# Second expert layer of a two-block kernel: own sums behind own down products, the last pair gathered in round 2, the first triple's gate products ahead of its up products

## What is computed

```python
def hier_moe(x, ...):                 # x: 256 tokens x 1024
    g_sel = argmax(x @ router_group_w + b)          # one of 4 groups
    top_logit, top_local = top_k(e_logits[g_sel], 2) # 2 of its 8 experts
    weight = p_group * softmax(top_logit)
    # every token goes to its 2 of 32 experts
    hid = silu(xb @ expert_w_gate[e]) * (xb @ expert_w_up[e])   # 1024 -> 256
    yb = hid @ expert_w_down[e]                                 # 256 -> 1024
    y = zeros.at[token].add(yb * weight)
x = layer_norm(DEEPNORM_ALPHA * x + hier_moe(x), ln2_w, ln2_b)
```

## Time and profile before

| | |
|---|---|
| time, three runs | 1296.77, 1297.43 (median), 1298.36 us |
| profiled execution: its time, its span | 1297.06 us, 1295.3 us |
| granted TensorE clock, mean | 0.940 |
| PE busy / PE weight loads / DVE / ACT / POOL | 1104.0 / 618.2 / 398.8 / 202.7 / 123.2 us |
| chain that ended last, by engine | PE 61%, DMA 31%, DVE 4%, ACT 2% |
| second experts' refills, rate of the 16 DMA engines in slices 34 to 39 of 40 (1068.6 to 1262.9 us) | 416, 421, 420, 420, 421, 419 GB/s |

### The profile page before, as it was taken

One profiled execution on the slowest core, in us unless ns is written; L12 is line 12 of the kernel. 1 busy time (PEld: TensorE's weight loads), 2 busy tenths in 40 slices (PEclk: granted clock), 3 DMA queues, 4 the chain that ended last, 5 costly groups with the idle time before them and its releaser, 6 DMA issues.

```text
span 1295.3 us, 19542 instructions
## 1 busy us (share of the span) xinstructions
PE 1104.0 (85%) x8698; PEld 618.2 (48%) x8698; DVE 398.8 (31%) x816; ACT 202.7 (16%) x420; POOL 123.2 (10%) x148
## 2 busy tenths in 40 slices
PE   7989997986667766776699999999999969998986
PEld 6645554432222222222264555888878544443432
DVE  4255843111001000100028827543185351011003
ACT  3221422010000000000000012211131032222121
POOL 0010000010003891000005610000000000000000
PEclk9999997999788778878899999999999989999988
DMA  9422848999999999999962353211313889999991
GB/s 331 150 90 107 351 197 332 427 427 428 427 429 427 426 428 427 428 427 428 414 221 98 130 211 105 107 67 67 132 65 130 327 332 416 421 420 420 421 419 45
DMA packets 62407, 377.45 MB, mean 291 GB/s; under 512 B 6128, under 2 KB 7664, under 8 KB 37104
## 3 DMA queue, kind: packets, MB, share of 16 engines
q1 hardware_dynamic: 60736, 369.64, 70.1%
q10 hardware_dynamic: 1584, 6.51, 1.4%
HBM read 375.09 MB, written 1.05 MB: 290 GB/s over the span
## 4 chain that ended last, share of the span: by engine, by line
PE 61%; DMA 31%; DVE 4%; ACT 2%; SPq 1%; issue 1%; DVEq 0%; ACTq 0%
DMA arena<-in_w_expert_up 21%; PE psum L489 11%; PE psum L492 9%; PE psum L2807 5%; DMA arena<-in_expert_w_up 4%; PE psum L1393 3%; PE psum L855 3%; PE psum L2273 3%; DMA arena<-in_w_expert_gate 3%; PE psum L1423 2%; PE psum L2495 2%; PE psum L2358 2%; PE psum L1102 2%; DMA arena<-in_w_expert_down 2%; PE psum L2818 2%; PE psum L2797 2%
## 5 line engine op out<-in xcount | busy, mean ns | idle before, releaser
L1393 PE MATMUL psum<-arena 128*32 128x256 f32 x2048 | 153.0, 449 | 91.3 <-DMA arena<-in_w_expert_up 54.5
L489 PE MATMUL psum<-arena 128*128 128x512 f32 x352 | 157.6, 598 | 3.2 <-ACT arena L526 1.6
L1393 PEld LDWEIGHTS psum<-arena 128*32 128x32 f32 x2048 | 70.8, 124 | 174.0 <-DMA arena<-in_w_expert_up 71.7
L1423 PE MATMUL psum<-arena 128*32 128x512 f32 x512 | 125.0, 640 | 17.2 <-DMA arena<-in_w_expert_down 11.9
L492 PE MATMUL psum<-arena 128*128 128x256 f32 x544 | 122.9, 382 | 1.0 <-ACT arena L1830 1.0
L492 PEld LDWEIGHTS psum<-arena 128*128 128x128 f32 x544 | 101.5, 189 | 16.9 <-issue 2.2
L489 PEld LDWEIGHTS psum<-arena 128*128 128x128 f32 x352 | 64.8, 190 | 81.4 <-issue 81.1
L2807 PE MATMUL psum<-arena 128*32 128x512 f32 (+2 forms) x672 | 82.4, 624 | 13.1 <-DMA arena<-in_expert_w_up 10.3
L1423 PEld LDWEIGHTS psum<-arena 128*32 128x32 f32 x512 | 31.4, 116 | 98.6 <-issue 71.1
L1454 DVE TENSOR_TENSOR arena<-arena,psum 128x256 f32<-128x256 f32 x16 | 6.8, 422 | 221.3 <-ACT arena L1437 221.3
L1561 POOL TENSOR_TENSOR arena<-arena 128x16 f32<-128x16 f32 (+6 forms) x64 | 43.6, 682 | 151.7 <-DMA arena<-in_ssm_bc 146.8
(11 more groups left out here) (482 smaller groups left out, 1229.7 us busy)
## 6 DMA issues: line engine op xcount, KB each, us to landing
arena<-in_w_expert_gate SPq DMA_DIRECT2D x32, 2048.0 KB, 25.2
arena<-in_w_expert_up SPq DMA_DIRECT2D x32, 2048.0 KB, 26.2
arena<-in_w_expert_down SPq DMA_DIRECT2D x31, 2048.0 KB, 25.0
arena<-in_w_in SPq DMA_DIRECT2D x21, 2048.0 KB, 8.9
arena<-in_expert_w_gate SPq DMA_DIRECT2D x32, 1024.0 KB, 19.5
arena<-in_expert_w_up SPq DMA_DIRECT2D x32, 1024.0 KB, 21.6
arena<-in_expert_w_down SPq DMA_DIRECT2D x32, 1024.0 KB, 23.3
arena<-in_w_out SPq DMA_DIRECT2D x4, 2048.0 KB, 7.8
```

What stands on the lines that cost most here:

```text
L489: mm = pe.matmul(o, lhs[:, k, sub * P:(sub + 1) * P], w[:, k, :], start=(k == 0), stop=(k == kt - 1))
L1393: mm = pe.matmul(ps[32 * c:32 * c + 32], xin[:, e, k], w[:, j, 256 * n:256 * n + 256], start=(k == 0), stop=(k == KD - 1))
L1423: mm = pe.matmul(y_ps[at:at + 32, 512 * n:512 * n + 512], hid_T4[:, j, half], w[:, j, 512 * n:512 * n + 512], start=(half == 0 and j == 0) ...
```

## The change

- Each `r2_tokens` signal now comes after each of the eight scalings. PE's wait in front of `either` is gone; in `few` the first products wait for one token part at a time, in `many` the wait for all eight stands before `begin_sums`.
- Round 0's products (`first_products_in`) are 256 wide: first all of gate, signalling the new `m2_gate`, then all of up, signalling `m2_in`. SP's `ins(2)` sends its three gate loads after `m2_gate`, its three up loads after `m2_in`.
- In rounds 0 to 8 `add(u)` comes directly after `out_of(u)`; there is nothing left between `gather_for(u+1)` and `turn_of(u)` (but `begin_sums` in round 0).
- The pair's tokens are gathered in round 2 (`SPARE`), between `turn_of(2)` and `out_of(2)`, into `x_sb`, which is free by then; its matrices are made on DVE in the same round. `nth` renumbers the counts of the semaphores for that.
- Round 9 has no gather and no add of the round before: `into(9)`, `turn_of(9)`, `into(10)`, `out_of(9)`, `turn_of(10)`, `add(9)`, `out_of(10)`, `add(10)`.

```diff
                     if k % 2 == 0:
                         act.wait_ge(*count("r2_gathered", k // 2 + 1))
-                    ins = take_tokens(act, tokens2[0], k, bank(k // 2)[:, (k % 2) * P:(k % 2 + 1) * P])
-                ins.then_inc(inc("r2_tokens"), 1)
+                    take_tokens(act, tokens2[0], k, bank(k // 2)[:, (k % 2) * P:(k % 2 + 1) * P]).then_inc(inc("r2_tokens"), 1)
...
+            SPARE = 2
+            nth = lambda u: SPARE + 2 if u == LAST else u if u <= SPARE + 1 else u + 1
...
+            x_words = x_sb.rearrange("p t d -> p (t d)")
+            pair_tokens = x_words[:, 0:KD * P].rearrange("p (k c) -> p k c", k=KD)
+            pair_chosen, pair_picked = (x_words[:, KD * P + NT * P * j:KD * P + NT * P * (j + 1)] for j in range(2))
...
                     def ins(u):
+                        if u == 2:
+                            sp.wait_ge(*count("m2_gate", 1))
+                            for e in experts_of(u):
+                                load_in(sp, e % W2_SLOTS, e, (0,))
+                            sp.wait_ge(*count("m2_in", 1))
+                            for e in experts_of(u):
+                                load_in(sp, e % W2_SLOTS, e, (1,))
+                            return
...
+                def first_products_in(tokens, groups):
+
+                    for j in range(2):
+                        for k in range(KD):
+                            if j == 0:
+                                pe.wait_ge(*count("r2_tokens", k + 1))
+                            for g, w in enumerate(groups):
+                                mm = pe.matmul(in_ps[32 * g:32 * (g + 1), FF2 * j:FF2 * (j + 1)], tokens[:, k, 32 * g:32 * (g + 1)],
+                                               gates_up(w)[:, k, j], start=(k == 0), stop=(k == KD - 1))
+                        mm.then_inc(inc(("m2_gate", "m2_in")[j]), 1)
...
                     def gather_for(u):
-                        pe.wait_ge(*count("m2_picks", u))
-                        if u > 1:
-                            pe.wait_ge(*count("m2_y0", u - 1))
-                            pe.wait_ge(*count("m2_y1", u - 1))
+                        pe.wait_ge(*count("m2_picks", nth(u)))
...
                     def out_of(u):
-                        if u < LAST:
-                            pe.wait_ge(*count("m2_tokens", u + 1))
-                        else:
-                            pe.wait_ge(*count("m2_y0", u))
-                            pe.wait_ge(*count("m2_y1", u))
                         pe.wait_ge(*count("m2_turned_out", u + 1))
...
-                    for u in range(LAST):
+                    for u in range(LAST - 1):
                         groups[u] = weights_of(u)
                         into(u)
                         gather_for(u + 1)
                         if u == 0:
                             begin_sums(pe)
-                        else:
-                            add(u - 1)
                         turn_of(u)
-                        if u == LAST - 1:
-                            groups[LAST] = weights_of(LAST)
-                            into(LAST)
+                        pe.wait_ge(*count("m2_tokens", nth(u + 1)))
+                        if u == SPARE:
+                            gather_for(LAST)
+                            pe.wait_ge(*count("m2_tokens", nth(LAST)))
                         out_of(u)
+                        add(u)
+                    groups |= {LAST - 1: weights_of(LAST - 1), LAST: weights_of(LAST)}
+                    into(LAST - 1)
+                    turn_of(LAST - 1)
+                    into(LAST)
+                    out_of(LAST - 1)
                     turn_of(LAST)
                     add(LAST - 1)
                     out_of(LAST)
...
+                    pe.wait_ge(*count("r2_tokens", KD))
                     begin_sums(pe)
                     pair_units(pe, unit)
 
-                pe.wait_ge(*count("r2_tokens", 1))
                 either(pe, few, many)
...
                         sigmoid(u)
-                        tokens_from(tokens2[(u + 1) % 2], 2 * u)
-                        take_turned(u)
+                        if u < LAST - 1:
+                            tokens_from(tokens_of(u + 1), 2 * nth(u + 1) - 2)
+                        if u == SPARE:
+                            take_turned(u)
+                            tokens_from(tokens_of(LAST), 2 * nth(LAST) - 2)
+                        else:
+                            take_turned(u)
```

More of the change, by code:

```diff
@@ L2706, in experts2, with load_in @@
             in_ps, turned_ps, y_ps = bank(4), bank(5), banks(6, 2)
-            def load_in(sp, s, e):
-                for j, name in enumerate(("expert_w_gate_2", "expert_w_up_2")):
+            x_words = x_sb.rearrange("p t d -> p (t d)")
+            pair_tokens = x_words[:, 0:KD * P].rearrange("p (k c) -> p k c", k=KD)
+            pair_chosen, pair_picked = (x_words[:, KD * P + NT * P * j:KD * P + NT * P * (j + 1)] for j in range(2))
+            tokens_of = lambda u: pair_tokens if u == LAST else tokens2[u % 2]
+            chosen_of = lambda u: pair_chosen if u == LAST else chosen2[u % 2]
+            picked_of = lambda u: pair_picked if u == LAST else picked[u % 2]
+            def load_in(sp, s, e, parts=(0, 1)):
+                for j in parts:
+                    name = ("expert_w_gate_2", "expert_w_up_2")[j]
                     src = D[name][bass.ds(e, 1)].rearrange("o d n -> (o d) n")
@@ L2837, in into @@
                         if u:
-                            pe.wait_ge(*count("m2_tokens", u))
+                            pe.wait_ge(*count("m2_tokens", nth(u)))
                         for e in experts_of(u):
                             pe.wait_ge(*count(f"m2_in_loaded{e % W2_SLOTS}", 32 * (e // W2_SLOTS + 1)))
-                        products_in(tokens2[u % 2], groups[u])
+                        (products_in if u else first_products_in)(tokens_of(u), groups[u])
                     def gather_for(u):
-                        pe.wait_ge(*count("m2_picks", u))
-                        if u > 1:
-                            pe.wait_ge(*count("m2_y0", u - 1))
-                            pe.wait_ge(*count("m2_y1", u - 1))
+                        pe.wait_ge(*count("m2_picks", nth(u)))
                         for k in range(KD):
-                            mm = gather2(pe, k, y_ps[:, k * P:(k + 1) * P], chosen2[u % 2])
+                            mm = gather2(pe, k, y_ps[:, k * P:(k + 1) * P], chosen_of(u))
                             if k % 4 == 3:
@@ L2854, in turn_of @@
                         pe.wait_ge(*count("m2_hid", u + 1))
-                        turn(hid[u % 2], picked[u % 2])
+                        turn(hid[u % 2], picked_of(u))
                     def out_of(u):
-                        if u < LAST:
-                            pe.wait_ge(*count("m2_tokens", u + 1))
-                        else:
-                            pe.wait_ge(*count("m2_y0", u))
-                            pe.wait_ge(*count("m2_y1", u))
                         pe.wait_ge(*count("m2_turned_out", u + 1))
@@ L2999, in few @@
                             choose(dve, chosen2[(u + 1) % 2], u + 1).then_inc(inc("m2_picks"), 1)
[L3000 removed]
+                            dve.wait_ge(*count("m2_picks", nth(u + 1)))
                             weigh(u + 1)
[L3002 to L3005, removed]
+                        if u == SPARE:
+                            choose_pair(pair_chosen, PAIRS - 1, 0).then_inc(inc("m2_picks"), 1)
+                            dve.wait_ge(*count("m2_picks", nth(LAST)))
+                            weigh_pair(pair_picked, pair_chosen, PAIRS - 1)
                         multiply(hid[u % 2], u + 1)
```

## The result

| | before | after |
|---|---|---|
| median of 8 runs | 1297.91 us (1295.17 to 1301.18) | 1301.72 us (1300.82 to 1303.69) |
| ratio | | 1.0034, 95% interval 1.0020 to 1.0048 |
| profiled execution: time, span | 1297.06, 1295.3 us | 1302.64, 1300.7 us |
| start of the first gather of the second experts | 1051.93 us | 1054.25 us |
| from there to the end of the span | 243.37 us | 246.45 us |

The kernel became slower by 0.34%. The forecast was 1299.4 us; 1301.7 lies in its range (1295.0 to 1302.8), and its sign was right, its size (+ 2.0, measured + 3.8) about half.

A forecast was written before the change was run, and what follows sets the result against it. The prediction took DMA to bound the kernel from round 7 on, and PE's chain after the change: 1057.4 + 197.1 + 42.8 = 1297.3, with 1.76 around it and 0.37 for the median 1299.4 us, range 1295.0 to 1302.8.

The forecast's parts named there:

- The bound changes hands: PE ready for into(9) at 1254.5, ten microseconds after its weights (1244.5): PE's own chain, not DMA, is the bound.
- The start: into(0) begins at the gather's end, 1057.4, register load and branch covered by the gather: 2.75 us come back.
- A round: Rounds 1 and 3 to 8 on PE: 6.99 + 6.20 + 4.45 + 3.44 = 21.08 us, before 19.0.
- ACT's order: Turned copy waits behind ACT's token scalings: down products 6.20 us after the gather's start instead of 5.11, costing 1.09.
- Round 2: With the pair's gather, down products start 11.16 us after the gather's start; the round takes 26.04 us.
- Tail: From into(9) to the end: into(9) 6.99, uncovered turn 2.1, into(10) 7.02, the rest 26.7; 42.8 us in all.
- The sum: Start, rounds and tail: 1057.4 + 197.1 + 42.8 = 1297.3 against a span of 1295.3, + 2.0 us.
- the forecast's own case: PE's chain bounds from start to end: 1299.4 us, range 1297.6 to 1301.2, a quarter above 1300.0; chance 0.56.
- rival 1: Branch before into(0) not covered by the gather: start at 1059.3, + 1.9 us, time 1301.3; chance 0.20.
- Holes of DMA: In the DMA stream the hole of 3.9 us closes; new ones of 2.2 before ins(3) and 2.2 before ins(5).
- Rival 2: DMA stays the bound if PE's rounds were 20 us or less: out_of(9) at about 1261, time 1290; chance 0.12.
- Rival 3: Gaps of 1.8 and 0.8 us in rounds lower PE's clock: 1302.4 with one fall, 1326 with one every round; chance 0.07.

The follow-up runs named there:

- e7: The kernel before with one edit, the add of rounds 0 to 8 following its own down products: 1302.32 us, ratio to before 1.0039.
- e4: Changed kernel, but SyncE issues triple 2's gate and up loads together after all of round 0's first products: 1303.3 us, ratio to before 1.0029.
- e2: Changed kernel, but VectorE instead of ScalarE copies the turned matrices out of PSUM in rounds 0 to 8: 1296.64 us, ratio to before 0.9988.
- e3: Changed kernel with PE's wait for all eight token parts back before the register load and branch: 1305.43 us, ratio to before 1.0047.
- e1: Changed kernel with add(u-1) back between gather and turn in rounds 1 to 9: 1288.81 us, ratio to before 0.9922.
- e8: Changed kernel with the adds back between gather and turn, except round 8's, which follows its own down products: 1287.45 us, ratio to before 0.9921.
- e5: Changed kernel with the pair's gather back in round 9, between into(9) and turn_of(9): 1299.99 us, ratio to before 1.0012.

## Why the forecast held, and where its size was off

- *The bound changes hands.* Right, and the main point. Before, the chain named DMA from round 7 on. PE's rounds, made 2.2 us longer (21.16 against 18.99), left no wait for DMA; e7 shows this for the one edit alone, e4 that the stream's hole is then without price, e2 and e3 that whatever PE gains or loses arrives at the end.
- *The start.* Right in kind: register load and branch are covered by the gather. The gather's length was taken from one execution: 5.80 to `into(0)` instead of 5.47, + 0.33. That is chance: the seven kernels with the early start had 5.10 to 6.69 there.
- *A round.* 21.16 against 21.08. Two errors cancel in part: an add behind a wait costs 3.63 to the next start, not 3.44 (nine times, + 1.7), and the down products start at 6.07, not 6.20 (seven times, - 0.9), since ACT's copy begins 0.1 before the end of its scalings. The forecast put the whole loss before the down products down to ACT's order. It is 0.96 (6.07 against 5.11), and e2 splits it: 0.54 is the order, 0.42 the wait for the scalings themselves (5.53 against 5.11).
- *Round 2.* 26.04, 1104.89 to 1130.93 in the profile after; the forecast said 26.04. That it agrees to the last digit is luck: the down products start 10.96 after the gather's start, not 11.16, and the add costs 0.19 more.
- *Tail.* 42.84 against 42.8; the open turn of round 9 is there with 1.42 idle.
- *The sum.* + 3.08 in the expert part where + 2.0 was forecast: + 0.33 of the gather and + 0.75 of the rounds. The term that was mis-sized is the add behind a wait, taken from a full stream. The medians differ by 3.81; the 0.7 left over is within the interval (2.6 to 6.2 us). 0.1 of it lies outside the span (time less span is 1.94 on average after and 1.80 before; the forecast took 1.76 for both), the rest is open.
- *The chances.* 1301.7 is above 1300.0, the case "slower by over 0.2%", which had 0.42; "the same" had 0.45. It is also above the range of the forecast's own case (1297.6 to 1301.2) and nearest to the time of rival 1 (1301.3). By the time alone the two could not be told apart; the rows decide.
- *Holes of DMA.* The old one closed as forecast; new ones of 2.2 and 2.2 forecast, 2.6 and 2.2 seen.
- *Rival 1* (branch not covered) is refuted by the start's rows: `into(0)` has no idle time before it, where 1.90 us would have stood.
- *Rival 2* (DMA stays the bound) would have needed rounds of 20 us. It describes e1 instead, where the down products of round 9 start at 1261.87 (about 1261 in the rival) and the time is 1288.81 (1290).
- *Rival 3*, the clock: it was at its full level (1.00) in every stretch from 1062 to 1270, and 0.99 on average over 1060 to 1301 (0.96 before over 1060 to 1296). So two short gaps in every round did no harm here, and for gaps of 1.78 and 0.81 the trace does not agree with the warning of the Trainium skill (TensorE: Matmul & The Clock Gate, A second HAM failure mode: psum-queue depth-cycling).

What the forecast did not say, and its own sums could have: with the sums left in their place, the change would have gained. The chain before had 15.8 us of waits for DMA and half clock. The early start and the pair's gather in round 2 won 6.0 of them and 2.6 at the start (e1, 0.78% faster than before); the moved sums took more than that away again.

## What to carry to other kernels

Where two engines are near balance, sum each one's chain with the change in it before pricing anything: here 2.2 us a round on PE were enough to make a prefetch, rightly built, worth nothing. An operation that stands between a producer and its consumer is cover even if it looks like a delay; before moving it, name what it covered on each engine (here ACT's scalings and its order, DVE's copy, and the multiplications of round 9) and count the rounds. Test the parts of a bundled change in a table of two by two: a part that gains in one column may lose in the other.

## What was not expected of the hardware

The length of an idle time alone did not tell whether TensorE's clock would be at its half level (1.2 of 2.4 GHz) afterwards. In e1 a product after 3.20 us of idleness took 7.07 us (granted clock 1.00 in 1220 to 1223), and one after 3.17 took 8.65 (0.50 in 1242 to 1244). In e3 one after 2.96 took 8.70; before the change, after 2.75, 7.07. In e8 even 2.61 were followed by a stretch at half clock (0.50 in 1219 to 1221):

```profile
1217.03 8.77 PE L2823 MATMUL psum<-arena 128*32 x64 [2.61 <-DMA arena<-in_expert_w_up]
```

The first gather, the same 32 matmuls in every kernel, took 5.17 (e5) to 6.76 us (e8), as part of it ran at half clock. The mean granted clock up to the start of `into(0)` was 0.72 in e5 (5.10 us), 0.63 in the changed kernel (5.80) and 0.54 in e8 (6.69): time and clock multiply to 3.6 to 3.7 in each, the 3.67 us of a later gather at full clock. So the clock accounts for the whole spread of the gather. As its start is spread over 4.5 us too, a difference of 1 to 2 us between whole runs of this kernel can only be read from the times of its parts.
